# Attention jobs ahead of the weight split, and twenty products elsewhere, in a two-block transformer kernel

## What is computed

```python
# block 1
a = rmsnorm(x, attn_norm); proj = a @ w_in          # splits for 4 HGRN2, 6 fox and 6 MoBA heads, fox gate logits
oa = hgrn2_mixer(...)                                # 4 heads
ob = softmax(q k^T * d^-.5 + fq[:, None] - fk[None, :]) v   # fox, q and k normalised per head, f = cumsum(log_sigmoid)
oc = softmax(q k^T * d^-.5 - slope * dist) v         # MoBA: 256 tokens are one block, so plain causal with slopes
h = x + concat(oa, ob, oc) @ w_out
h = h + (gelu(conv(c @ w_gate)) * (c @ w_up)) @ w_down      # c = rmsnorm(h), D_FF 5632
h = h + sigmoid(e @ w_ple_gate) * (p @ w_ple_proj)          # e = rmsnorm(h)
# block 2
mod = silu(c) @ w_mod + b_mod                        # 2048 -> 6 x 2048: shifts, scales, gates
h = rmsnorm(x) * (1 + sc1) + sh1; proj = h @ w_in_2
o_a = 16 sliding-window heads with sinks and a bias table; o_b = 8 MLA heads (latents, rotary part)
x = x + g1 * (concat(o_a, o_b) @ w_out_2)
u = relu(norm(x) modulated @ w_ff1); x = x + g2 * (u*u @ w_ff2)   # 8192 wide
return rmsnorm_2(x)
```

## Time and profile before

| | |
|---|---|
| median of three runs | 2400.34 us |
| the profiled execution: device time | 2399.3 us |
| its span, first to last instruction | 2397.6 us |
| PE busy | 2337.4 us (97%), clock granted 0.992 of full |
| DVE busy | 1940.7 us (81%) |
| ACT busy | 1178.0 us (49%) |
| POOL busy | 109.0 us (5%) |
| the chain that ended last | PE 89%, DVE 7%, ACT 2% |

### The profile page before, as it was taken

The page is one execution under the profiler, slowest core; times in us unless marked ns, Lnnn a source line. Parts: engine busy times, 40 slices in busy tenths (PEclk is TensorE's granted clock), DMA queues, the critical chain, the costliest instruction groups (busy, mean ns, idle before and its releaser), DMA issues.

```text
span 2397.6 us, 38235 instructions
## 1 busy us (share of the span) xinstructions
PE 2337.4 (97%) x13766; PEld 2032.2 (85%) x13766; DVE 1940.7 (81%) x3144; ACT 1178.0 (49%) x1697; POOL 109.0 (5%) x208
## 2 busy tenths in 40 slices
PE   7999999999999999999999999999999999999997
PEld 6888787888888888888888897788988888888886
DVE  6987787889988889898989866778777777777777
ACT  5544444565545454454456666545644434434432
POOL 0000010001000000000000000000000000000000
PEclk9999999999999999999999999999999999999998
DMA  7456666458888878788775652436455545555552
GB/s 284 172 189 228 234 237 214 156 203 302 275 280 277 282 270 288 260 298 277 277 267 176 213 197 89 151 130 223 182 193 179 191 181 189 189 180 192 179 191 88
DMA packets 86244, 514.43 MB, mean 215 GB/s; under 512 B 9669, under 2 KB 10229, under 8 KB 36944
## 3 DMA queue, kind: packets, MB, share of 16 engines
q1 hardware_dynamic: 57312, 407.93, 47.6%
q0 software_dynamic: 28640, 104.24, 13.0%
q10 hardware_dynamic: 144, 0.26, 0.0%
HBM read 510.27 MB, written 2.13 MB: 214 GB/s over the span
## 4 chain that ended last, share of the span: by engine, by line
PE 89%; DVE 7%; ACT 2%; issue 2%; DMA 1%; SPq 0%; DVEq 0%; ACTq 0%; POOLq 0%
PE ps L532 46%; PE ps L533 23%; PE ps L530 4%; PE ps L525 2%; PE ps L526 2%; PE ps L527 2%; PE ps L529 2%; DVE wl L1363 2%; PE ps L589 2%; ACT wh L863 1%; PE ps L598 1%; DVE x L1415 1%; PE ps L617 1%; DVE modraw L1431 0%; PE ps L566 0%
## 5 line engine op out<-in xcount | busy, mean ns | idle before, releaser
L863 ACT ACTIVATE wh<-raw 128x1024 fp32r<-128x1024 f32 x768 | 810.7, 1057 | 728.9 <-PE ps L530 481.2
L1363 DVE TENSOR_TENSOR wl<-raw,wh 128x1024 fp32r<-128x1024 f32 x768 | 938.0, 1223 | 249.4 <-ACT wh L863 233.4
L532 PE MATMUL ps<-xs,wh 128*128 128x512 f32 x2907 | 1050.1, 402 | 19.7 <-DVE wl L1363 13.2
L533 PE MATMUL ps<-xs,wl 128*128 128x256 f32 x2907 | 817.9, 281 | 0.0
L532 PEld LDWEIGHTS ps<-xs,wh 128*128 128x128 f32 x2907 | 549.5, 189 | 150.2 <-DVE wl L1363 14.0
L533 PEld LDWEIGHTS ps<-xs,wl 128*128 128x128 f32 x2907 | 552.2, 190 | 10.2
L1431 DVE CUSTOM_DVE_ANT_0 modraw<-modraw,cb 128x1024 f32<-128x1024 f32 x192 | 233.2, 1218 | 4.4 <-DMA modraw<-in_wmod 4.4
L1415 DVE SCALAR_TENSOR_TENSOR x<-ps,mod,x 128x256 f32<-128x256 f32 x320 | 154.8, 484 | 88.4 <-PE ps L530 82.7
L532 PE MATMUL ps<-xc,wh 128*128 128x512 f32 x616 | 222.0, 399 | 0.0
L532 PE MATMUL ps<-hs,wh 128*128 128x512 f32 x608 | 218.8, 398 | 1.9 <-DVE x L1413 1.9
L533 PE MATMUL ps<-xc,wl 128*128 128x256 f32 x616 | 173.3, 281 | 0.0
(11 more groups left out here) (286 smaller groups left out, 2983.0 us busy)
## 6 DMA issues: line engine op xcount, KB each, us to landing
raw<-in_w SPq DMA_DIRECT2D x383, 1024.0 KB, 5.0
modraw<-in_wmod POOLq DMA_DIRECT2D x192, 512.0 KB, 4.5
x<-in_x SPq DMA_DIRECT2D x4, 512.0 KB, 8.7
tbias<-rel_rows POOLq DMA_DIRECT2D x4, 512.0 KB, 6.0
out_dram<-mix SPq DMA_DIRECT2D x4, 512.0 KB, 2.6
raw<-in_w SPq DMA_DIRECT2D x2, 512.0 KB, 7.9
cb<-c_silu POOLq DMA_DIRECT2D x1, 1024.0 KB, 8.6
hmask<-in_hmask SPq DMA_DIRECT2D x1, 512.0 KB, 17.3
```

The costliest lines, as they stand in the source:

```text
L532: nc.tensor.matmul(out[:, :], hi[:, w], pair, start=s, stop=e)
L533: m = nc.tensor.matmul(out[:, 0:T], lo[:, w], xh, start=False, stop=e, skip_group_check=e)
L863: nc.scalar.activation(wh[:, h % HS, :], raw[:, u % RAW, (h % 2) * 1024:(h % 2 + 1) * 1024], ACT.Copy).then_inc(s_round, 1)
L1363: nc.vector.tensor_tensor(wl[:, h % HS, :], raw[:, (h // 2) % RAW, (h % 2) * 1024:(h % 2 + 1) * 1024], wh[:, h % HS, :].bitcast(F32), ALU. ...
```

## The change

- `half` gets a part `pre`, which runs before the bank is emptied and before `sub`. The DVE steps of all attention jobs move there (`fox_jobs`, `moba_jobs`, `swa_jobs`, `mla_jobs`). PE's and ACT's places stay. MoBA and MLA jobs end one half earlier.
- Mixed heads are split one by one: ACT and DVE each handle a head as soon as its output is there. Blocks 0 to 7 of `out` go to a new place `xm`, in stage C; the six MoBA and the eight MLA heads go in the first part of their products. The twelve value transposes are done four at a time, at halves 30 and 34 of stage C and half 1 of `out`.
- 20 products leave stage C (33 to 13); each of the four loop passes gets four more, the second input product four more (halves 2 to 9, one each). The eight of `out2` go from its second to its first part. POOL issues six loads ahead of `cossin` and `perm`.
- Head norms: sums go to 44 rows (0 to 11 and again 32 to 43), root and reciprocal run over 44 rows, DVE makes a pair (rounded, remainder) of them, and the spread is one fp32r matmul of 44 rows by a selector `pick`. DVE sets up `strip2` and `pick` at the start of stage C.
- The query's gate sum leaves the fox scores: PE transposes it twice, ACT copies it to `fqt`, and DVE adds it as the per-row operand of L1550.
- The last down product is `joined`, and DVE adds once (`add_joined`). The low half of `px` is made one half earlier, ahead of a product.

```diff
-            def half(before=None, after=None):
+            def half(before=None, after=None, pre=None):
+                if pre:
+                    pre()
                 if before:
                     dve.wait_ge(s_used, c.val("h", c.n["h"]))
                     before()
...
-        LATE_MODS = 14
+        LATE_MODS = 18
-        moba_steps = lambda i: share(C_H + JOB_LAG, i, MOBA_J, 2 * U_OUT)
+        moba_steps = lambda i: share(C_H + JOB_LAG, i, MOBA_J, 2 * U_OUT - 1)
-        mla_steps = lambda i: share(MLA_H + JOB_LAG, i, MLA_J, 2 * U_OUT)
+        mla_steps = lambda i: share(MLA_H + JOB_LAG, i, MLA_J, 2 * U_OUT - 1)
+        out_taken = lambda steps, i: [j - JOB_LAG for j in steps(i) if j >= JOB_LAG]
...
             return dict(scores=lambda t: [(sec[:, S0 + h, qt(t)], sec[:, S0 + B_H + h, 0:keys(t)]),
-                                          (fnp[:, 0, qt(t)], sel.to_broadcast([B_H, keys(t)])),
                                           (sel.to_broadcast([B_H, P]), fnp[:, 1, 0:keys(t)])],
...
+            mod_loads(POOL_MODS + MOD_SLOTS, POOL_MODS + 8)
             pool.wait_ge(s_ssq, 4 * N_ATTN2 + 4)
...
-                            mm = nc.tensor.matmul(PS[4 + j % 2][:, q * T:(q + 1) * T], spread(2 * j + q, 2 * B_H),
-                                                  hrs[:, :], start=True, stop=True)
+                            mm = nc.tensor.matmul(PS[4 + j % 2][:, q * T:(q + 1) * T], spread2(2 * j + q),
+                                                  hpair[:, :], start=True, stop=True)
...
             def moba(i):
-                if i == 0:
+                if i == 1:
                     pe.wait_ge(s_scl, SCALED["out"])
-                    pe.wait_ge(s_oe, J_MOBA)
-                    for g in range(C_H // 2):
-                        v_transposes(3, sec[:, S1 + 2 * C_H:S1 + 3 * C_H, :], g)
-                    pe.wait_ge(s_hn, 12)
+                    pe.wait_ge(s_vt, 4)
+                    moba_v(2)
...
+                    link(nc.vector.reciprocal(hrs[:, :], hrs[:, :]))
+                    link(nc.vector.tensor_copy(hpair[:, :], hrs[:, :]))
+                    low = slice(32, HROWS)
+                    nc.vector.tensor_tensor(hpair[low, :], hrs[low, :], hpair[low, :].bitcast(F32), ALU.subtract
+                                            ).then_inc(s_hr, 1)
...
-            fulls(U_C, keep(S1), lambda j: 1 + (j >= 3), fox)
+            fulls(U_C, keep(S1), lambda j: 1 <= j < 14, fox, jobs=fox_jobs)
...
+            def add_joined(ks):
+                for k in ks:
+                    nc.vector.tensor_tensor(x[:, k, :], bank()[:, 0:T], x[:, k, :], ALU.add).then_inc(s_evac, 1)
+                dve.wait_ge(s_evac, c.n["b"])
```

More of the change, by code:

```diff
@@ L179, in build @@
         strip = small[:, 40:40 + 4 * B_H - 1]
+        fqt = small[:, 24:24 + 2 * B_H]
         gsc = at("gsc", [P, 2], 187.375)
@@ L585, in job_step @@
                         pe.wait_ge(s_lg, J - 1)
+                    pairs = [d["scores"](t) for t in range(2)]
                     for t in range(2):
-                        pairs = d["scores"](t)
-                        for q, (l, r) in enumerate(pairs):
-                            m = nc.tensor.matmul(PS[4 + J % 2][:, part(t)], l, r, start=q == 0, stop=q == len(pairs) - 1)
+                        for q in range(len(pairs[0])):
+                            m = nc.tensor.matmul(PS[4 + J % 2][:, part(t)], *pairs[t][q], start=q == 0,
+                                                 stop=q == len(pairs[0]) - 1)
                     m.then_inc(s_sc, 1)
@@ L1090, in fox @@
                 head_norm(1, S1, i - MOBA_N)
+                if i - 1 in MOBA_V:
+                    v_copy(3, MOBA_V[i - 1], 7 - MOBA_V[i - 1] % 2)
+                if 0 <= i - MIX_AT < 4:
+                    his("C", XMIX["out"][2 * (i - MIX_AT):], [mix[:, 2 * (i - MIX_AT) + k, :] for k in range(2)])
             for u in range(U_C):
@@ L1458, in eights @@
                         dve.wait_ge(s_oe, jobs_done)
-                    for k in range(8 if split else 8 * part, 8 * part + 8):
-                        lo(XS[name] + k, XMIX[phase][k], mix[:, k, :])
                     for i in range(2 * U_OUT):
                         half((lambda: add_blocks([i - 1], gate)) if i else None,
-                             after=lambda: (second(i) if part else between(i)))
+                             after=lambda: (second(i) if part else between(i)), pre=None if part else lambda: jobs(i))
                     tail(lambda: add_blocks([KB - 1], gate))
```

177 lines of the change are left out of this document (123 added, 54 removed).

## The result

The changed kernel takes **2373.02 us** (median, 2370.51 to 2374.47); the kernel before, run beside it, 2399.98 (2397.83 to 2402.98). The ratio is 0.9891, 95% interval 0.9879 to 0.9904. The prediction was 2360 with a range of 2347 to 2376. So the sign and the range hold, but 27 us were gained where the sum had 40. The profiled execution has a span of 2372.7 against 2397.6: 24.9 us.

The account below looks back on a forecast made before the run. TensorE (PE), busy 2337.4 of 2397.6 us, was taken as the bound. The terms summed to 40.0 us: 2399.3 - 40.0 + 1.0 (profiled execution to median) = 2360.3, called 2360, range 2347 to 2376.

Parts of the forecast that it names:

- Gate pair: Six fox jobs: each loses a matmul pair of 0.86 us to DVE; net gain 4.9 us after transposes.
- Clock in the first fox job: Half clock from 299.4 to 302.8, after the mostly 6-row matmuls, cost 1.7 us; half booked as gain, 0.9.
- Head roots: Head-norm spreads: 24 matmuls at 0.20 instead of 0.50 us, less 1.0 for DVE's pace; gain 6.2 us.
- Products moved: 20 modulation products leave stage C for loop and second input product; price 0, bounds 19 and 2 us.
- Heads split as they come: First half of the first output product: splits, transposes and waits shrink from 10.2 us; gain 6.0.
- Rival (d): 44-row products stay slow (6.2 us back), and transposes in stage C bring two half-clock drops of 1.7; 2370, chance 0.07.
- L1493: PE's waits for mixed heads' low halves in the second part of both output products go; gain 2.9 us.
- Quads: Last down product with joined products: 16 of 32 DVE additions go; gain 2.7 us, bounds 1 and 4.
- Scores ahead: Between 1447.6 and 1505.3: DVE's job precedes addition and subtraction, cutting PE's waits and half clock; gain 8.5 us, bounds 4 and 10.
- End of the second output product: Eight products leave 1603.8:1649.7, so DVE regains its lead before the last feed-forward; gain 6.4 us, bounds 3 and 6.7.
- (a): DVE's waits come back elsewhere, so scores save 3.5, roots 3 and quads 1 us; 2370, chance 0.20.
- Rival (c): Slower: DVE waits at its queue's head for scores, MLA halves take 7.6 against 5.90 us; 2408, chance 0.03.

Follow-up runs that it names:

- fox_pair_on_PE: in2_as_before with the fox jobs' query gate sum as a matmul pair on PE again, which puts the loop at instruction 6596; 2385.41 us (0.9939).
- in2_time_only: in2_as_before with four extra DVE operations of a product's size, without loads, in the second input product; 2365.69 us (0.9856).
- in2_as_before: The changed kernel with the second input product's modulation products and load order as before, four products left over going to the second output product; 2366.22 us (0.9863).
- pad42_after: The changed kernel with 42 fulfilled-wait instructions ahead of everything on PE, so the loop starts at 6590; 2386.72 us (0.9942).
- positions_and_in2: in2_as_before with pads that put PE's loop at instruction 6632 and DVE's at 953, as in the kernel before; 2358.77 us (0.9829).
- loop_24_products: positions_and_in2 with the loop's added products moved out, 12 to stage C and 4 to the PLE gate, 24 a pass left; 2359.40 us (0.9830).

## Why the prediction was right, and where its sum was not

The time lies in the stated range, and in part by luck: 21.2 us were lost in two places that the sum had at 0, and the other terms gained some 6 more than their 40, 1.4 of it by chance. By its own steps, with what each term measured (no run took out the head roots, the early splits, px, the quads or the eight products by themselves: their numbers are differences of stretches):

- **Gate pair, 4.9:** 4.1. The step that failed is the price of a pair, taken from start to start (0.32 and 0.54); it is 0.68 a job in place of 0.86. The bound from below, which left 0.12 of each for the hand-over, was the better value (0.62 a job, 3.7 in all; the prediction says 3.8).
- **Clock in the first fox job, 0.9 (half of 1.7):** the window went, 1.5 of the 5.6. Its cause, as the prediction had it (the 6-row matmuls), is not borne out: `fox_pair_on_PE` has them and has no window in its one profiled execution. What brought it stays open.
- **Head roots, 6.2:** 6.6 (3.15 + 3.41). A spread matmul takes 0.22 where 0.20 was put, DVE's pace costs less than the 1.0 put. Two groups of four in the kernel after, the second held up by DVE:

```profile
265.94 0.73 PE L579 MATMUL ps<-hpair,pick 44*128 44x256 f32 x4
269.95 1.07 PE L579 MATMUL ps<-hpair,pick 44*128 44x256 f32 x4 [0.25 <-DVE sec L1587]
```

  By the drain at a change of tiling mode that the Trainium skill's TensorEngine Tiling (Array Packing) page, Key Properties, speaks of, some of the old price would have stayed. The four of 265.94 follow each other at 0.15, 0.03 above the full rows; what is left of a drain is small here.
- **Products moved, 0 with bounds of 19 in the loop and 2 in the second input product:** this step failed. Its reason was right as far as it went (DVE's time: four more operations changed nothing in `in2_time_only`), but a product is an operation and a load of 512 KB. In the second input product DVE's wait for the loads cost 7.1, over the bound; in the loop products and loads together cost 4, with 8 to 17 us of DVE's waits for the loads where there had been none. The prediction looked at POOL's queue only for who stands behind the loads (cossin), not for how long a load takes to land (5.6 us) once its slot is free.
- **Heads split as they come, 6.0:** 7.4 in half 106, 0.4 of it lost again where the transposes went (98 to 101), less than their 1.4. Rival (d) had two half-clock windows there by what the Trainium skill's page TensorE: Matmul & The Clock Gate, PE-mode transpose, says of transposes. None came in stage C of the kernel after (PEclk 1.00 in its rows above).
- **L1493, 2.9:** 3.5 (1.64 + 1.84). **px, 1.5:** 1.7. **Quads, 2.7:** 2.2, and 1.7 more in the stretch behind them, where PE had waited 1.3 us.
- **Scores ahead, 8.5:** 9.5 in halves 461 to 479, and the size came from the right waits. The mechanism was named by its smaller part: "earlier by the subtraction and the take before it, 1.2 + 0.4" is worth 1.1 us there (2.2 with the first output product), and the reciprocals, scalings and low halves that stood between them the rest. The prediction's price was near, by luck as far as its 1.6 goes: it bounded the term by the waits.
- **End of the second output product, 6.4:** 6.6. Four of the eight products came back there in `in2_as_before` at 0.5 us, so not every product taken out was worth the same; I read it as DVE's lead being used up or not when the stretch ends.
- **What no step had:** PE's code. 84 instructions fewer ahead of the loop put its body over one block more: 9.6 us between the profiled executions, 7.6 by the medians. It is not part of what the change does at all; the same change with 84 pad instructions, 42 of them spread, does not have it. And 1.4 us ahead of stage C are chance: a half-clock window at about 217 us comes in some executions and not in others, whatever the kernel.

Sum: 46.6 us gained (with that 1.4), 13.4 and 7.8 lost, and 0.9 in everything else (0.4 where the transposes went, the rest in the last feed-forward): 24.5 of the 24.9 of the spans. The forecast lay at 2360 because the terms were nearly all right; its own list of what would make it wrong named "a pass of the loop grows" and "the half clock appears at new places", and both happened. The rivals (a) and (d), 2370 each, had the number but not the place: DVE's waits did come back elsewhere, but as waits for loads and code; and four new half-clock windows came, but behind idle gaps of PE, three at the loop's jump and one at 1430.2, not among transposes. Rival (c) (whose 1.8, 4.12, 0.4 and 1.2 add up to 7.5, not 7.6) left no sign: PE waits for wl in no half with a job. The kernel that undoes the refetch and the loss in the second input product, at 2359, is where the forecast was, with 4.3 us of the loop's loss still in it.

## What to carry to other kernels

A change is also a change of where every later instruction stands. When a loop that was not touched gets longer, look at the instruction queues in a window of one pass before looking for contention; if one kernel fetches there and the other does not, count the loop's instructions and the blocks that they touch, and pad. When an operation is moved into a gap of its engine, price its load as well: from the moment its slot comes free to its landing, against the time until the operation that reads it; time to spare is not lead to spare. And an operation that another engine waits for gains by what it passes: list all that stood between its operand and it, not the one instruction that the change names.

## What the runs showed of the hardware that was not expected

- PE kept a loop of 1621 instructions (6.3 blocks of 16 KB) loaded over its passes from the one start at which it touches 7 blocks, and fetched it again in every pass from the four at which it touches 8: 6 against 33 or 34 packets. The refetch leaves PE idle for 1.0 to 3.5 us at a jump, and for 4.6 to 8.0 where the loop begins 42 or 48 instructions further on (`pad42_after`, `fox_pair_on_PE`); where half clock follows, 1.7 us or more come on top, and with gaps of 1.6 to 2.6 in `in2_as_before` none followed.
- DVE fetches code at every jump back in all kernels, even the fastest, 2 packets of 8 KB one behind the other, and stands 3.2 us at best and 6.4 at worst. In the kernels with 24 products a pass the first packet starts 2.1 to 2.4 us behind the back-edge, in those with 28 at 2.8 to 5.6.
- A load of 512 KB into a slot just freed lands 3.8 to 8.4 us after its issue in the second input product (5.6 in the median). With two slots, DVE waits for such loads at 28 products a pass of the loop (11.9 us in 14 waits in `positions_and_in2`) and for none at 24 (`loop_24_products`).
- An instruction of two waits that are already fulfilled costs PE about 0.11 us at its program's start (172 against 84: 26.7 and 17.4 us to the first matmul), and nothing that could be measured when three to a half stand among full matmuls.
- The loop with refetches takes 551.3 to 555.7 us in five kernels that share its code and place; with all code in time it takes 542.29 in three.
